# Two queues for the operand loads of a feed-forward product: spilled hidden blocks by ScalarE, weight quarters by SyncE

## What is computed

```
x   = layer_norm(ALPHA * x + mix, ln1_g, ln1_b)
hid = square(relu(x @ ffn_w1))                     # 1024 x 4096
x   = layer_norm(ALPHA * x + hid @ ffn_w2, ln2_g, ln2_b)
x   = x + sigmoid(x @ ple_gate_w) * (p @ ple_w)
```

## Time and profile before

| what | value |
|---|---|
| median of 3 runs | 2103.36 us (2103.15 to 2104.1) |
| profiled execution, its own time | 2104.21 us |
| its span, first to last instruction | 2102.5 us |
| TensorE clock granted | 1.000 over the span |
| busy: TensorE / VectorE / ScalarE / GpSimd | 99% / 59% / 37% / 35% |
| DMA | 287.17 MB, mean 137 GB/s |

### The profile page before, as it was taken

One profiled execution on the slowest core, in us unless ns is written; L12 is line 12 of the kernel. 1 busy time (PEld: TensorE's weight loads), 2 busy tenths in 40 slices (PEclk: granted clock), 3 DMA queues, 4 the chain that ended last, 5 costly groups with the idle time before them and its releaser, 6 DMA issues.

```text
span 2102.5 us, 25078 instructions
## 1 busy us (share of the span) xinstructions
PE 2089.8 (99%) x9605; PEld 1734.6 (83%) x9605; DVE 1238.4 (59%) x1619; ACT 788.4 (37%) x1165; POOL 730.7 (35%) x493
## 2 busy tenths in 40 slices
PE   9999999999999999999999999999999999999999
PEld 8888788888888888888888888888888888888887
DVE  5744776565666657565543352675556566666563
ACT  3112464445543334531211101455444544334530
POOL 5112157777502000221432222267777512000220
PEclk9999999999999999999999999999999999999999
DMA  5111124344599555311121111124434599554221
GB/s 186 38 63 46 35 81 150 139 153 156 184 348 390 202 190 180 110 36 36 41 81 41 53 48 40 41 81 155 153 139 160 182 373 380 189 192 170 96 86 40
DMA packets 180819, 287.17 MB, mean 137 GB/s; under 512 B 12800, under 2 KB 71260, under 8 KB 180700
## 3 DMA queue, kind: packets, MB, share of 16 engines
q1 hardware_dynamic: 180000, 285.26, 39.4%
q10 hardware_dynamic: 700, 0.31, 0.1%
HBM read 221.56 MB, written 63.96 MB: 136 GB/s over the span
## 4 chain that ended last, share of the span: by engine, by line
PE 67%; DVE 2%; POOL 1%; issue 1%; ACT 1%; DMA 1%; SPq 0%; ACTq 0%; POOLq 0%; DVEq 0%
PE bank_a L1853 12%; PE bank_a L1854 12%; PE bank_a L1855 12%; PE bank_b L1853 10%; PE bank_b L1855 10%; PE bank_b L1854 10%; POOL op_lo L1023 1%; PE bank_a L1892 1%; DMA w_raw<-in_ffn_w_dram 1%; PE bank_b L1892 1%; POOL op_sum L1096 0%; DVE hop_lo L1594 0%; DVE xt_lo L1395 0%; ACT op_hi L1251 0%; DVE wop_lo L1597 0%
## 5 line engine op out<-in xcount | busy, mean ns | idle before, releaser
L1009 POOL TENSOR_TENSOR w_lo<-raw,w_hi 128x512 fp32r<-128x512 f32 x148 | 205.4, 1421 | 866.1 <-ACT w_hi L1117 865.9
L1853 PE MATMUL bank_a<-xt_hi,w_hi 128*128 128x512 f32 x640 | 251.3, 393 | 0.1
L1855 PE MATMUL bank_a<-xt_hi,w_lo 128*128 128x512 f32 x640 | 249.2, 389 | 0.0
L1854 PE MATMUL bank_a<-xt_lo,w_hi 128*128 128x512 f32 x640 | 249.1, 389 | 0.0
L1221 ACT CAST hop_hi<-h_raw 128x1024 fp32r<-128x1024 f32 x112 | 117.8, 1052 | 243.4 <-PE bank_a L1855 145.5
L1594 DVE TENSOR_TENSOR hop_lo<-h_raw,hop_hi 128x1024 fp32r<-128x1024 f32 x112 | 137.5, 1228 | 118.3 <-ACT hop_hi L1221 118.1
L1855 PE MATMUL bank_a<-wop_hi,hop_lo 128*128 128x512 f32 x512 | 199.2, 389 | 0.0
L1853 PE MATMUL bank_a<-wop_hi,hop_hi 128*128 128x512 f32 x512 | 199.2, 389 | 0.0
L1854 PE MATMUL bank_a<-wop_lo,hop_hi 128*128 128x512 f32 x512 | 199.2, 389 | 0.0
L1117 ACT CAST w_hi<-raw 128x512 fp32r<-128x512 f32 x148 | 82.3, 620 | 284.5 <-PE bank_a L1855 154.7
L1023 POOL TENSOR_TENSOR op_lo<-op_sum,op_hi 128x512 fp32r<-128x512 f32 x112 | 166.1, 1501 | 10.6 <-ACT op_hi L1251 6.3
(11 more groups left out here) (198 smaller groups left out, 4741.2 us busy)
## 6 DMA issues: line engine op xcount, KB each, us to landing
w_raw<-in_ffn_w_dram SPq DMA_DIRECT2D x144, 512.0 KB, 6.5
h_raw<-h_spill SPq DMA_DIRECT2D x112, 512.0 KB, 5.5
h_spill<-h_tile SPq DMA_DIRECT2D x170, 256.0 KB, 2.3
w_raw<-in_ffn_w_dram SPq DMA_DIRECT2D x112, 256.0 KB, 3.3
raw<-in_od_w_in_dram SPq DMA_DIRECT2D x48, 256.0 KB, 2.9
raw<-in_ple_gate_w_dram SPq DMA_DIRECT2D x32, 256.0 KB, 3.4
h_spill<-h_tile2t SPq DMA_DIRECT2D x28, 256.0 KB, 2.0
raw<-in_ev_w_in_dram SPq DMA_DIRECT2D x24, 256.0 KB, 3.1
```

The source lines that it names most:

```text
L1009: pool.tensor_tensor(lo, raw[:, n % NRAW, :], hi.bitcast(F32), ALU.subtract).then_inc(lo_split, 1)
L1853: pe.matmul(dst, s_hi, m_hi, start=first, stop=False, skip_group_check=on_top)
L1854: pe.matmul(dst, s_hi, m_lo, start=False, stop=False, skip_group_check=on_top)
L1855: return pe.matmul(dst, s_lo, m_hi, start=False, stop=last, skip_group_check=on_top)
```

## The change

From item 8 (the ninth) to item 47 the load of `h_raw` is issued by ScalarE instead of SyncE, in both layers: 40 loads a layer, 80 in all. `load_item` on SyncE is cut in two, and SyncE keeps only the part for `w_raw` for these items, at the same places of the plan. ScalarE gets a `load_hid` of its own with the waits that SyncE had (`hop_low` of item n - 7, the spill of the block, or `first_out` for block pair 0), and does it at the start of its prep stage: at prep 5 for items 8 to 11, at prep i for item i + 6 when i > 5. Items 48 to 55 and items 0 to 7 are loaded as before.

```diff
--- before.py
+++ after.py
@@ -812,6 +812,11 @@
 
             def load_item(layer, i):
 
+                load_hid(layer, i)
+                load_w2(layer, i)
+
+            def load_hid(layer, i):
+
                 a, last = ahead[layer], FFN_BLOCKS - 1
                 form, _ = ITEMS[i]
                 p, role = a.pair(i), FORMS[form][1]
@@ -833,6 +838,11 @@
                 slot, _ = a.hop_landed(i)
                 src = h_dram[layer, 2 * p:2 * p + 2, role].rearrange("k p s -> p k s")
                 sp.dma_start(h_raw[a.hop_chunk(i)][:, :, :], src).then_inc(h_in[slot], 16)
+
+            def load_w2(layer, i):
+
+                a, last = ahead[layer], FFN_BLOCKS - 1
+                form, p = ITEMS[i][0], a.pair(i)
                 for n, quarter in enumerate(FORMS[form][2]):
                     load = a.first_load[i] + n
                     before = a.w_before(load)
@@ -972,7 +982,9 @@
                             .then_inc(first_out, 16)
                 if st.kind == "prep":
                     for n in range(8, 12) if st.item == 4 else (st.item + 7,) if st.item > 4 else ():
-                        if n < len(ITEMS):
+                        if n < LAST_FORM:
+                            load_w2(st.layer, n)
+                        elif n < len(ITEMS):
                             load_item(st.layer, n)
                 if st.kind == "a" and st.first and st.blk == 0:
 
@@ -1130,6 +1142,21 @@
                     act.wait_ge(t_summed, 8 * layer + base + m + 1)
                     act.copy(pair_of(t_hi[k], m), pair_of(t_raw[k], m)).then_inc(t_high, 1)
 
+            def load_hid(layer, i):
+
+                a, form = ahead[layer], ITEMS[i][0]
+                p, role = a.pair(i), FORMS[form][1]
+                act.wait_ge(ahead_dve, a.hop_low[a.hop_before(i)])
+                if p:
+                    act.wait_ge(spill_out[role], a.spilled(role, 2 * p + 1))
+                elif form in ("m1", "m2", "m4"):
+                    act.wait_ge(spill_out[role], a.spilled(role, 1))
+                else:
+                    act.wait_ge(first_out, 64 * (layer + 1))
+                slot, _ = a.hop_landed(i)
+                src = h_dram[layer, 2 * p:2 * p + 2, role].rearrange("k p s -> p k s")
+                act.dma_start(h_raw[a.hop_chunk(i)][:, :, :], src).then_inc(h_in[slot], 16)
+
             def values(st):
 
                 for k in range(len(st.js) if st.kind == "turn" else 2):
@@ -1210,6 +1237,9 @@
                 if st.kind == "prep":
                     a, i = ahead[st.layer], st.item
                     k, form = a.slot(i), ITEMS[i][0]
+                    for n in range(8, 12) if i == 5 else (i + 6,) if i > 5 else ():
+                        if n < LAST_FORM:
+                            load_hid(st.layer, n)
                     if a.user_before(i) is not None:
                         name, value = item_done(a, a.user_before(i))
                         act.wait_ge(sem_of[name], value)
```

## The result

The changed kernel takes 2120.38 us (median of 6 runs, 2117.91 to 2124.86) against 2103.7 us (median of 6 runs of the kernel before): 16.7 us slower, a ratio of 1.008 with a 95% interval of 1.007 to 1.009. The forecast had the sign, 2109.4 us as the time, and a range that ended at 2112.0.

A forecast was written before the change was run, and what follows sets the result against it. TensorE, busy for 99% of the 2102.5 us span, was taken as the bound. Stalls at item 9 of 3.3 us (layer 0) and 2.7 us (layer 1), other parts 0, added 6.0 us: 2109.4 us, range 2103.0 to 2112.0.

The forecast's parts named there:

- the slack of item 9: Time between item 9's weights being ready and TensorE needing them: 2.97 us in layer 0, 3.45 us in layer 1.
- The sum: Predicted TensorE stalls at item 9 in both layers, 3.3 + 2.7 = 6.0 us, with the other parts at 0.
- Stall 2.7 us: Layer 1, TensorE at item 9: weights ready at 1727.1 us, due at 1724.35.
- psum: 4.75 us: VectorE's psum work after item 8's weights, taken to last as before (610.49 to 615.24 us).
- `wop_lo` ends 3.50 us after `t` starts: VectorE, last steps of item 9's weights: duration taken from the kernel before, 617.66 to 621.16 us.
- No stall. From there ... the lag dies out: Item 11 ready at 635.1 us, due at 638.3; then six loads (8.1 us) serve two items (10.88 us).
- The upper bound of 9.8 us: Item 9 stalls with one more load ahead at both places: 5.1 and 4.7 us.
- (a): Rival, no change, 2103.4 us: loads served by age whatever their queue, or second queue raises the rate; 0.30 with (d).
- (b): Rival, faster, 2102.6 us: W2's loads arrive earlier because ScalarE's loads take only idle DMA turns; chance 0.03.
- (c): Rival, slower, 2116 us: ScalarE held at issues while the queue is full, preps 5 to 8; chance 0.05.
- (d): Rival, 2103.4 us: ScalarE reaches prep 5 late and the load order stays; 0.30 together with (a).

The follow-up runs named there:

- The run with one queue: Kernel before, no load on ScalarE: SyncE issues the `h_raw` loads in the order they go through in the changed kernel, up to item 15; 2120.7 us.
- the run from item 24 on: Changed kernel, but ScalarE issues the `h_raw` loads only from item 24 on and SyncE keeps items 8 to 23; 2104.25 us.
- the three shorter leads: Changed kernel, but ScalarE issues each load two, three or four items ahead instead of six; 2106.7, 2108.9 and 2112.7 us.
- The run without GpSimd's subtraction: Changed kernel, but VectorE does the first subtraction of each m6 item itself in place of GpSimd; 2114.53 us.
- The stall put alone into the kernel before: Kernel before, but TensorE's item 9 also waits for the low parts of items 10 and 11; 2118.03 us.
- its waits alone: Kernel before, all loads on SyncE, but ScalarE waits for `hop_low` at prep 5 and later as in the changed kernel; 2103.51 us.

## Why the prediction was right or wrong

**The mechanism was right.** Loads of `h_raw` slip ahead of W2's and spend the slack of item 9. Its working holds in the main by its own steps: four issues at 586 to 588 us (585.3 to 588.3 measured), ready time of item 5 at 601.8 (600.9), of item 8 at 618.7 (617.65), GpSimd's start at 620.5 to 621.9 (619.5), item 9 of layer 0 stalled by 3.3 us (3.6). With the 0.26 us of this execution taken off, the two ready times and GpSimd's start (against the lower end of its range) came 1.1 to 1.3 us earlier than forecast, about one load of 1.355 us. One reading of the working was wrong: a load on ScalarE's queue was to be through in at most 5.5 us, and those issued at 598.67 to 605.92 us took 7.0 to 7.1. The run with one queue shows that it is the order, the run from item 24 on shows where, and the three shorter leads show the dose.

**The sum was 6.0 us; the medians show 16.7, the profiled execution 20.6.** In the terms of that execution 0.3 us were missing in layer 0's stall, 3.6 in layer 1's, 3.2 at item 24, and 7.8 for the clock: 20.9 with the 6.0. Three steps of it failed.

*"Stall 2.7 us" in layer 1* was 6.3. The step that failed is "psum: 4.75 us" and "`wop_lo` ends 3.50 us after `t` starts": both durations were read in the kernel before, where VectorE sits idle while GpSimd subtracts. Once the two overlap, an instruction takes 2.2 us more; in layer 1 two did. With the 11.27 us off by which this execution runs later there, `t` starts at 1724.95 in place of 1723.6 (psum, 1.35 us), and `wop_lo` takes 3.38 in place of 1.22 (2.16 us): 3.5 of the 3.6 that are missing. In layer 0 one did, and the 3.3 us came out near the mark by luck: the slowed addition's 2.2 us were offset by item 8 being ready 1.3 us earlier than forecast. The run without GpSimd's subtraction shows that the long instructions are its doing.

*No price for the clock.* The sum took a wait at its own length. Behind each of the three waits the matmuls ran at the lower of the two clocks for a while: 7.8 us in the profiled execution. The stall put alone into the kernel before shows it apart from all else.

*"No stall. From there ... the lag dies out"* was wrong, though item 11 did start on time with 0.23 us in hand. The reckoning looked at item 11 and at the DMA rate, but not at VectorE, whose work for items 10 to 27 stands before the flush of m6, with five more slowed instructions and late loads in it: item 24 waited 3.0 us. How that wait divides between the two stays open. The DMA rate, too, fell to 159 and 204 GB/s in two stretches of 5 us after item 9's start was due, so less of the lag was caught up than the reckoning had.

**The bounds.** The upper bound of 9.8 us was "one more" load ahead at both places. The count was about one load too high in layer 0 (GpSimd's start came 4.1 us later than before, not 5.4 to 6.8) and near in layer 1 (5.2 us), which by itself would have made the stalls shorter than forecast. So this bounded the wrong thing; what was unknown were the durations under overlap and the clock.

**The rivals.** (a), no change at 2103.4, is out: item 5's load came 3 us later with four loads beside it, and the two queues moved 214 and 210 packets while both held loads. The rule that the prediction set beside it (the Trainium skill, page "DMA: Bandwidth & Descriptors", section "Issuing engines are not separate DMA queues") is about the issuing time and the engines all DMAs share. There the trace agrees, 387 GB/s before and 387 to 393 after; that rule says nothing of the order. The order is what cost the time. (b) is out with it. (c), ScalarE held at an issue, had the best number (2116) for a wrong reason: its issues took 0.37 to 0.45 us, but for the first four of each layer, which took 3.0 us together, and its waits alone cost nothing. (d) is out: q10 moved what was forecast.

**Left open.** Why the waits differ from execution to execution (2117.9 to 2124.9 us) was not taken apart, and each wait was read in one profile per kernel. What share of item 24's wait comes from slowed instructions and what from late loads was not separated, nor whether ScalarE's in-order waits, free while loads are on time, add to it when they are late. Whether the lower clock follows a wait differed between waits of like length (1.97 and 2.23 us), and no run shows why. A separate order of psum and the flush was not tried.

## What to carry to other kernels

Before a stream of loads is moved to a queue of its own, look for a stretch in which the DMA engines are full: there a queue is not a lane, it is a place in the order, and what was issued first because it is needed first loses its turn to whatever is issued early next to it. Keep one queue, or limit the second to a short lead, until the engines have room; here, from item 24 on, the same move cost nothing that the time shows.

When a delay is carried through a chain of engines, durations read while the neighbour was idle don't hold once the two overlap, and a wait of TensorE can cost more than its length: 1.75 to 3.0 us more behind those of 3.0 to 6.1 us in the changed kernel, 0.1 us more behind one of 2.2 us.

## What was not expected of the hardware

A VectorE `tensor_tensor` on 128x1024 float32, 1.22 us alone, takes 2.9 to 3.4 us when GpSimd's `tensor_tensor` on the same shape (2.4 us) starts beside it; GpSimd's own then takes 2.65 to 3.3 us. In the pairs shown the one that starts second is the longer by what is left of the other. In the kernel before that was GpSimd, once a layer and cheaply, since VectorE's instruction was half through. VectorE:

```profile
674.02 1.22 DVE L1597 TENSOR_TENSOR wop_lo<-w_raw,wop_hi 128x1024 fp32r<-128x1024 f32 x1
```

GpSimd:

```profile
674.65 2.84 POOL L1050 TENSOR_TENSOR w_raw<-w_raw,w_raw 128x1024 f32<-128x1024 f32 x1 [3.01 <-DMA w_raw<-in_ffn_w_dram]
```

Behind item 24's wait the matmuls of 128x512 take 0.62 to 0.76 us each from 714.57 to 720.25 us, and start 0.43 us apart in place of 0.23; one wait of 3 us cost another 3.0 in that way.
